# Output projection of the second attention layer: order of its first loads, and which engine forms its first remainders

## The chip, the cores and the metric

The kernel runs on one core of a Trainium2 chip. The metric is the time of one execution on the device, in microseconds. Three runs of the kernel before gave 1376.13, 1377.06 and 1377.77 us, a median of 1377.06 us. The core has a matrix engine (PE, TensorE), VectorE (DVE), ScalarE (ACT), GpSimd (POOL) and SyncE (SP, which here only issues DMAs). Each works through its own instructions in order, and they wait for one another on semaphores. Sixteen DMA engines carry the transfers of all queues.

## The reference

Two blocks over 512 tokens of width 1024. What matters here is the second layer of the first block, attention over 16 heads from shared latent keys and values, and the output projection at its end, the last line:

```python
def _mla_layer(x, w_in, q_norm, w_uq, w_out, k_nope, k_rope, v):
    b, s, _ = x.shape
    hproj = x @ w_in
    q_lat, gate = hproj[..., :Q_LORA], hproj[..., Q_LORA:]
    q = (_rms_norm(q_lat, q_norm) @ w_uq).reshape(b, s, H_B, QK_NOPE + QK_ROPE)
    q_nope = q[..., :QK_NOPE]
    q_rope = _rope(q[..., QK_NOPE:], ROPE_BASE_B)
    o = _causal_block_attention(q_nope, q_rope, k_nope, k_rope, v).reshape(b, s, WIDTH_B)
    return (o * jax.nn.silu(gate)) @ w_out
...
def first_block(x, ...):
    x = _retention_layer(...)                  # layer 0, then residual and layer norm
    x = _mla_layer(x, ..., *shared)            # layer 1, then residual and layer norm
```

A retention layer stands ahead of it. The second block behind it has a pooling mixer, neighbourhood attention and an MLP (its up and down projections).

## The kernel before

**Arithmetic.** Every fp32 operand is split in two parts: `hi`, the value rounded to the matrix engine's fp32r format, and `lo`, the remainder. A product is three matmuls, hi·hi, hi·lo and lo·hi (`split_dots`, L651 to L653). ACT rounds (`copy`, `weights_hi`, `operand_hi`), and DVE or POOL subtracts the rounded value from the original (`lo_of`, `weights_lo`, `operand_lo`, `split_lo`). So before each product a weight panel (128x2048, 1 MB) is loaded, ACT rounds it in two halves of 128x1024, and DVE or POOL forms the two remainders; the same happens to the operand from the activations (128x1024, one instruction each).

**The projections as seven products.** A large projection is done in the manner of Strassen: seven block products in place of eight, with sums of blocks as operands and sums of weight blocks as weights. The projection named `BO` (the last line of `_mla_layer`) has two panels to a product, so 14 panels, d = 0 to 13. In this text "product d" is what PE does with panel d, 24 matmuls of 512 columns. Panels 0 and 1 are plain weight blocks. Panels 2, 3 and later ones are sums of blocks, which lie ready in the DRAM tensor `tsum`.

**The sums of weights.** They are formed while attention runs: ACT copies a block into `tsum` by DMA, and POOL issues a DMA that adds another block or sum to it in DRAM (`sum_step`, issued at L872; 1 MB each, 8 KB to a packet). Each of the last sums (`DN`, for the down projection much later) waits in POOL until the sum ahead of it has landed (`add_to_sum`, which waits on `t_sum`). Of `DN`'s sums, number 10 was issued ahead of the last attention panel's remainders, in the loop over `k`, and number 11 behind the remainders of `BO`'s panel 0.

**Attention in pairs of heads.** Eight passes of `pairs`, two heads in each. A pass ends with: scores of the second head, exponentials (ACT) and normalisation (DVE); the products for the gate; the transposes of the probabilities, whose copies ACT makes as `pt_hi` and DVE as `pt_lo` (`turned`); the second head's attention on PE; the last adding up of the gate (`add_up(3)`), tanh on ACT, and the gated outputs `gt` on DVE (`gated`). SP stores `gt` to `o_spill` in DRAM (`store`). In the last pass the first operand and panel of `BO` are prepared between these steps.

**Operands of the projection.** `heads(c4)` loads four heads' outputs from `o_spill` into the tensor `bT` (1 MB) when their stores have landed. `heads(0)` and `heads(1)` serve products 0 and 1; the sums of blocks on DVE (`combine`, the tiles `comb` and `bT`) want `heads(2)` from product 4 and `heads(3)` from product 5 on. DVE waits for `heads(3)` ahead of the remainders of product 4. Stage buffers, `whi` and `wlo` rotate by three, so `seven_load` issues panel d when the remainders of panel d - 3 have been formed (`d_tlo`).

**Order on SP before.** `heads(0)`, `heads(1)`; then, when POOL has made the fourth sum of the gate (`m_ws`), panel 0; when the last attention panel's remainders are there (`w_lo`), panel 1, `heads(2)` and 1 MB of the residual `xres`; when PE has done the last gate product (`m_g`), panel 2, and panel 3 when panel 0's remainders are there; the two stores of the last pair, `heads(3)` behind them, and panels 4 to 13.

Of the kernel before, what the change touches and what calls it, by code (L numbers as in the profile page):

```python
# [32 lines left out]
PAIRS = HB // 2  # L33
# [45 lines left out]
BO = Seven(2, 14, 14, END + 8, 8, (33, 33, 33, 33), ((2, 3), (4, 5), (6, 7), (0, 1), (2, 3), (4, 5), (6, 7)))  # L79
UPN, UA = 16, 28  # L80
DN = Seven(4, UA + 2 * UPN, 28, END + 16, 16, (36, 36, 36, 40), ((0, 1), (2, 3), (4, 5), (6, 7), (0, 1), (2, 3), (4, 5)))
# [56 lines left out]
def program(nc, t, out):  # L138
    with ExitStack() as ctx:
# [7 lines left out]
        def sem(name):  # L147
            return ctx.enter_context(nc.semaphore(name))
# [175 lines left out]
        bld = xt_ld[0:4]  # L324
# [82 lines left out]
        m_s = sem("m_s")  # L407
# [54 lines left out]
        d_slo = sem("d_slo")  # L462
# [65 lines left out]
        def seven_stage(st, d):  # L528

            if st is DN:  # L530
                return third_set(d + 2)[0]
            i = own_panel(st) % 2
            return (stage[i], stage[1 - i], stage2)[d % 3]

        def seven_parts(st, d):

            if st is DN:
                hi, lo = third_set(d + 2)[1:]
            else:
                hi, lo = ((whi[0], wlo[0]), (whi[1], wlo[1]), (whi_a, wlo_a))[d % 3]  # L540
            return hi[:, 0:PAN], lo[:, 0:PAN]
# [30 lines left out]
        def seven_panel(st, f, g):  # L572

            if PLAIN[f] is None:
                return t["tsum"][st.sums + st.dq * SUMMED[f] + g, :, :]
            return block_panel(st, PLAIN[f], g)

        def block_panel(st, b, g):

            return t["w"][st.w + st.dq * b + g, :, 0:PAN]  # L580

        def sum_panel(st, i, g):

            return t["tsum"][st.sums + st.dq * i + g, :, :]
# [36 lines left out]
        def slot(x, k):  # L621

            return x[:, 512 * k:512 * k + 512]
# [35 lines left out]
        def _(sp):  # L659
# [42 lines left out]
            def seven_load(st, d):  # L702

                f, g = divmod(d, st.dq)
                if d >= 3:
                    sp.wait_ge(d_tlo, 2 * (st.at + d - 2))
                if g == 0 and SUMMED[f] is not None:
                    sp.wait_ge(t_sum, 16 * st.ready[SUMMED[f]])
                sp.dma_start(seven_stage(st, d)[:, 0:PAN], seven_panel(st, f, g)).then_inc(d_ld[(st.at + d) % 3], 16)
# [41 lines left out]
            def heads(c4):  # L751
                for e in range(2):
                    sp.wait_ge(m_st[e], 32 * (c4 + 1) + 16)
                sp.dma_start(bT[:, 4 * c4:4 * c4 + 4, :], t["o_spill"][4 * c4:4 * c4 + 4, :, :].rearrange(
                    "k p n -> p k n")).then_inc(bld[c4], 16)

            sp.wait_ge(m_kv, 4 * PAIRS)
            heads(0)
            heads(1)
            sp.wait_ge(m_ws, USED + 4 * PAIRS)  # L760
            seven_load(BO, 0)
            sp.wait_ge(w_lo, 2 * L0)
            seven_load(BO, 1)
            heads(2)
# [73 lines left out]
        def _(pool):  # L838
            def gate_sums():

                near = stage[M0 % 2]
                pool.wait_ge(landed[M0 % 2], LANDED[M0 % 2] + 16 * ((M0 + 2 - B0) // 2 + 1))
                pool.tensor_tensor(slot(near, G_S1), slot(near, G_S3), slot(near, G_S1), ADD).then_inc(m_ws, 1)
                pool.wait_ge(m_ws, USED + 1)
                pool.tensor_tensor(slot(near, G_S2), slot(near, G_S1), slot(near, G_A11), SUB).then_inc(m_ws, 1)
                pool.tensor_tensor(slot(near, G_S3), slot(near, G_A11), slot(near, G_S3), SUB).then_inc(m_ws, 1)
# [20 lines left out]
            def add_to_sum(st, i, g, src, copies, sums):  # L867

                pool.wait_ge(t_copy, 16 * (copies + 1))
                if sums:  # L870
                    pool.wait_ge(t_sum, 16 * sums)
                pool.dma_start(sum_panel(st, i, g), src, accum_op=ALU.add, max_dma_last_dim=8192).then_inc(t_sum, 16)  # L872

            def sum_step(st, i, copies, base):

                k, g = divmod(i, st.dq)
                if k == 0:
                    add_to_sum(st, 0, g, block_panel(st, 2, g), copies[0], 0)
                elif k == 1:
                    add_to_sum(st, 2, g, block_panel(st, 3, g), copies[0], 0)  # L880
                elif k == 2:
                    add_to_sum(st, 1, g, sum_panel(st, 0, g), copies[1], base + i)
                else:
                    add_to_sum(st, 3, g, sum_panel(st, 1, g), copies[1], base + i)

            def up_sum(k, g):

                pool.wait_ge(t_copy, 16 * ((12, 20)[k] + 1))
                pool.dma_start(t["usum"][k, g, :, :], t["w"][UP + g, :, 0:PAN], accum_op=ALU.add, max_dma_last_dim=8192
                               ).then_inc(t_sum, 16)  # L890

            def weights_lo(st, d):

                hi, lo = seven_parts(st, d)
                for b in range(2):
                    r = slice(b * PAN // 2, (b + 1) * PAN // 2)
                    pool.wait_ge(d_thi, 2 * (st.at + d) + b + 1)
                    pool.tensor_tensor(lo[:, r], seven_stage(st, d)[:, r], hi[:, r].bitcast(F32), ALU.subtract
                                       ).then_inc(d_tlo, 1)
# [45 lines left out]
            for k in range(4 * PAIRS):  # L945
                split_lo(M0 + k, PANEL if k % 4 == 0 else PAN)
                m = 3 * (k // 4) + k % 4
                if k % 4 == 2:
                    fourth_sum(k // 4)
                if k == 2:  # L950
                    pool.wait_ge(t_h, USED + 4)
                    pool.tensor_tensor(x_t4[1], xsum[:, 3], x_t4[0].bitcast(F32), ALU.subtract).then_inc(t_l, 1)
                if k % 4 == 3:
                    continue
                if m < 3:
                    up_sum(1, m)
                elif m == 3:
                    up_sum(1, 3)
                if 5 <= m < 13:
                    sum_step(BO, m - 5, (28, 28), 16)  # L960
                elif m >= 13:
                    sum_step(DN, m - 13, (36, 44), 24)
                if k == 0:
                    gate_sums()
            weights_lo(BO, 0)
            sum_step(DN, 11, (36, 44), 24)
            pool.wait_ge(w_lo, 2 * (L0 + 2))
            for p in range(L0 + 2, L0 + 6):
# [740 lines left out]
        def _(act):  # L1709
# [12 lines left out]
            def operand_hi(st, d):  # L1722

                f, g = divmod(d, st.dq)
                if d >= 3:
                    act.wait_ge(d_pe, st.op + d - 2)
                if SUM_OF[f] is not None:
                    act.wait_ge(d_sum, st.sums + (2 * UPN + 8 if st is DN else 0) + st.dq * SUM_OF[f] + g + 1)
                copy(operand_parts(st, d)[0], operand(st, d), d_shi)
# [318 lines left out]
            def pairs(it, last=False):  # L2048
                for s in range(2):
# [3 lines left out]
                    def c(per, k):  # L2053
                        return 2 * per * it + (per * s + k)
# [48 lines left out]
                    def next_hi(b):  # L2103
                        act.wait_ge(m_g, c(4, 7))
                        if last and s == 1:
                            if b == 0:
                                weights_hi(BO, 0)
                        else:
                            split_hi(p + 4, None, 0, PANEL, n, (b,))
# [16 lines left out]
                    for b in range(3):  # L2126
                        turned(1, b)
                    next_hi(1)
                    act.wait_ge(m_u, c(5, USED + 4))
                    tanh(0, first_t, bank[0][:, first_t])  # L2130
                    tanh(0, second_t, gate_kept[:, 0:HALF])
# [8 lines left out]

            for it in range(PAIRS // 2):
                pairs(it, it == PAIRS // 2 - 1)
            act.wait_ge(bld[1], 32)
            operand_hi(BO, 1)
            act.wait_ge(m_g, 4 * PAIRS + 4)
            weights_hi(BO, 1)
            for d in range(2, 14):
# [113 lines left out]
            for i in range(NS + 3):  # L2261
# [8 lines left out]
                if 2 <= i < NS + 2:  # L2270
                    m = i - 2
# [35 lines left out]
                if i >= 3:  # L2307
                    m = i - 3
# [102 lines left out]
        def _(dve):  # L2411
# [27 lines left out]
            def operand_lo(st, d):  # L2439

                hi, lo = operand_parts(st, d)
                dve.wait_ge(d_shi, st.op + d + 1)
                lo_of(lo, operand(st, d), hi, d_slo)
# [596 lines left out]
            def pairs(it, last=False, first=False):  # L3040
                for s in range(2):
# [90 lines left out]
                    add_up(2)  # L3132
                    for b in range(3):
                        turned(1, b)
                    if last and s == 1:
                        operand_lo(BO, 0)
                    dve.wait_ge(m_g, c(4, 8))
                    add_up(3)
                    gates(0, 0, first_t, bank[0][:, first_t])
# [11 lines left out]
                pairs(it)  # L3151
            own.leave(PAIRS // 2 - 1)
            pairs(PAIRS // 2 - 1, True)
            operand_lo(BO, 1)
            dve.wait_ge(m_g, 4 * PAIRS + 4)
            weights_lo(BO, 1)
# [103 lines left out]
            for i in range(NS + 2):  # L3260
                if i < NS:
# [5 lines left out]
                    for e in range(2):  # L3267
                        s = bank[4 + i % 2][:, e * 256:(e + 1) * 256].rearrange("p (r c) -> p r c", r=ROWS)
# [242 lines left out]
```

## Time and profile before

| | value |
|---|---|
| median of three runs | 1377.06 us (1376.13 to 1377.77) |
| the profiled execution | 1375.22 us, of which the span is 1373.1 us |
| PE busy | 1351.5 us (98%) |
| DVE busy | 1090.3 us (79%) |
| ACT busy | 766.7 us (56%) |
| POOL busy | 356.0 us (26%) |
| DMA | 265.65 MB, mean 193 GB/s |
| TensorE clock granted | 1.0 (2.4 GHz) through the span |

Times in rows are microseconds from the span's start. A row of a timeline gives the start, the duration, the engine, the line, the operation with output and input, the count, and in brackets how long the engine had been idle and what ended that. The stage of this text lies between 779 and 882 us: the end of the last pair of heads and the projection `BO`.

### The profile page before, as it was taken

What the parts mean: (1) busy time and instruction counts of PE and PEld (TensorE: products, weight loads), DVE (VectorE), ACT (ScalarE), POOL (GpSimd) and SP (SyncE); (2) the same over time, 40 slices, a digit from 0 to 9 for tenths busy, and PEclk for the clock granted to TensorE, in tenths of its full rate; (3) what the DMA queues carried; (4) which work ended last, traced back from release to release, by engine and by line L of the source; (5) the groups of instructions that cost most, each with busy time, mean ns of one, the idle gap of its engine ahead of it and who ended that gap; (6) DMA issues with size and microseconds to landing.
All of it is one profiled execution on the core that took longest, in us unless ns stands there. A gap on an engine that the chain in (4) does not pass through costs nothing. (4 is left out here: it accounts for less than half of the span.)

```text
span 1373.1 us, 19960 instructions
## 1 busy us (share of the span) xinstructions
PE 1351.5 (98%) x7596; PEld 1179.1 (86%) x7596; DVE 1090.3 (79%) x1751; ACT 766.7 (56%) x1233; POOL 356.0 (26%) x189
## 2 busy tenths in 40 slices
PE   9999999999999999999999989999999999999998
PEld 7788888888888998999899878777888999988887
DVE  7979787889967867776776689936876888889895
ACT  5453535457546444544455446648965666576554
POOL 2050414110045544544464410025304000000000
PEclk9999999999999999999999999999999999999999
DMA  6458675385377868795878797353122575456552
GB/s 270 168 177 232 192 202 186 126 281 206 132 222 180 260 212 250 226 286 119 261 231 264 201 307 295 125 205 120 66 85 78 161 212 165 150 183 213 200 190 101
DMA packets 55485, 265.65 MB, mean 193 GB/s; under 512 B 5744, under 2 KB 10480, under 8 KB 30576
## 3 DMA queue, kind: packets, MB, share of 16 engines
q1 hardware_dynamic: 38592, 166.71, 34.3%
q0 software_dynamic: 5760, 41.95, 15.6%
q10 hardware_dynamic: 11056, 55.97, 10.8%
q8 instruction: 47, 0.77, 0.2%
q14 instruction: 30, 0.25, 0.1%
HBM read 255.70 MB, written 92.80 MB: 254 GB/s over the span
## 5 line engine op out<-in xcount | busy, mean ns | idle before, releaser
L864 POOL TENSOR_TENSOR wlo<-stage,whi 128x1024 fp32r<-128x1024 f32 (+2 forms) x84 | 202.1, 2425 | 425.9 <-ACT whi L1717 339.6
L1720 ACT ACTIVATE whi<-stage 128x1024 fp32r<-128x1024 f32 (+2 forms) x155 | 148.2, 1002 | 108.0 <-PE bank L653 90.9
L2415 DVE TENSOR_TENSOR wlo<-stage,whi 128x1024 fp32r<-128x1024 f32 (+1 forms) x133 | 152.8, 1178 | 9.5 <-ACT whi L1720 9.5
L651 PE MATMUL bank<-xhi,whi 128*128 128x256 f32 (+1 forms) x428 | 133.8, 313 | 1.7 <-POOL wlo L1011 1.2
L653 PE MATMUL bank<-xhi,wlo 128*128 128x256 f32 (+1 forms) x428 | 132.9, 310 | 0.0
L652 PE MATMUL bank<-xlo,whi 128*128 128x256 f32 (+1 forms) x428 | 132.8, 310 | 0.0
L1717 ACT ACTIVATE whi<-stage 128x1024 fp32r<-128x1024 f32 (+2 forms) x90 | 89.5, 1037 | 20.2 <-issue 12.5
L651 PEld LDWEIGHTS bank<-xhi,whi 128*128 128x128 f32 x428 | 80.5, 188 | 7.2 <-DVE hid L2625 1.4
L652 PEld LDWEIGHTS bank<-xlo,whi 128*128 128x128 f32 x428 | 80.4, 188 | 5.0
L653 PEld LDWEIGHTS bank<-xhi,wlo 128*128 128x128 f32 x428 | 80.3, 188 | 5.0
L651 PE MATMUL bank<-whi,xhi 128*128 128x512 f32 (+1 forms) x204 | 78.3, 384 | 1.0 <-POOL wlo L864 0.6
L653 PE MATMUL bank<-whi,xlo 128*128 128x512 f32 (+1 forms) x204 | 77.3, 379 | 0.0
L652 PE MATMUL bank<-wlo,xhi 128*128 128x512 f32 (+1 forms) x204 | 77.2, 378 | 0.0
L913 POOL TENSOR_TENSOR wlo<-stage,whi 128x1024 fp32r<-128x1024 f32 x12 | 30.2, 2531 | 107.4 <-ACT whi L1720 107.4
L1720 ACT ACTIVATE whi<-oT 128x1024 fp32r<-128x1024 f32 x34 | 34.1, 1053 | 37.7 <-DVE oT L2876 17.9
L2090 ACT ACTIVATE prob<-bank,sm 128x512 f32<-128x512 f32 (+1 forms) x64 | 33.1, 523 | 35.1 <-DVE sm L3086 35.0
L651 PE MATMUL bank<-ql_hi,whi 128*128 128x512 f32 x120 | 47.0, 391 | 0.0
L653 PE MATMUL bank<-ql_hi,wlo 128*128 128x512 f32 x120 | 46.7, 389 | 0.0
L652 PE MATMUL bank<-ql_lo,whi 128*128 128x512 f32 x120 | 46.7, 389 | 0.0
L651 PEld LDWEIGHTS bank<-whi,xhi 128*128 128x128 f32 x204 | 38.3, 188 | 9.0 <-POOL wlo L864 1.4
L2415 DVE TENSOR_TENSOR wlo_a<-stage,whi_a 128x1024 fp32r<-128x1024 f32 x38 | 45.7, 1217 | 0.0
L653 PEld LDWEIGHTS bank<-whi,xlo 128*128 128x128 f32 x204 | 38.3, 188 | 7.0
(533 smaller groups left out, 4402.7 us busy)
## 6 DMA issues: line engine op xcount, KB each, us to landing
stage<-in_w SPq DMA_DIRECT2D x63, 1024.0 KB, 4.9
tsum<-in_w ACTq DMA_DIRECT2D x32, 1024.0 KB, 15.2
stage<-tsum SPq DMA_DIRECT2D x32, 1024.0 KB, 4.8
tsum<-in_w POOLq DMA_DIRECT2D x16, 1024.0 KB, 10.5
tsum<-tsum POOLq DMA_DIRECT2D x16, 1024.0 KB, 10.2
stage<-in_w SPq DMA_DIRECT2D x24, 512.0 KB, 4.7
stage<-in_w SPq DMA_DIRECT2D x8, 1152.0 KB, 6.2
usum<-in_w POOLq DMA_DIRECT2D x8, 1024.0 KB, 10.2
```

Source lines behind the costliest of these rows:

```text
L651: pe.matmul(dst, a_hi, b_hi, start=start, stop=False, skip_group_check=onto)
L652: pe.matmul(dst, a_hi, b_lo, start=False, stop=False, skip_group_check=onto)
L653: return pe.matmul(dst, a_lo, b_hi, start=False, stop=stop, skip_group_check=onto)
L864: pool.tensor_tensor(lo[:, to], stage[p % 2][:, r], hi[:, to].bitcast(F32), ALU.subtract).then_inc(w_lo, 1)
L913: pool.tensor_tensor(lo[:, r], a_staged(h, j)[:, r], hi[:, r].bitcast(F32), ALU.subtract).then_inc(g_plo, 1)
L1717: act.activation(parts(p)[0][:, to], stage[p % 2][:, r], ACT.Copy).then_inc(w_hi, 1)
L1720: act.activation(dst, src, ACT.Copy, scale=scale).then_inc(signal, 1)
L2090: act.activation(prob[:, at:at + w], bank[4 + q][:, 0:w], ACT.Exp, scale=-1.0, bias=sm[:, 1, 4 * e + q:4 * e + q + 1], accum_out=sm[:, 2, ...
L2415: dve.tensor_tensor(dst, src, hi.bitcast(F32), ALU.subtract).then_inc(signal, 1)
```

## The change

Four things are changed, all around the first products of `BO`.

1. SP issues the load of panel 0 between `heads(0)` and `heads(1)`, where it stood behind both.
2. The remainder of product 0's operand (`br_lo`) is formed by POOL, with a wait for the last scores of the last pair, where DVE formed it ahead of the last adding up of the gate. DVE now waits for it (`d_slo`) ahead of product 1's operand.
3. Sum 10 of `DN` is issued behind panel 0's remainders, directly ahead of sum 11.
4. ACT rounds product 1's operand ahead of the last tanh instructions, where it did so behind them.

```diff
             sp.wait_ge(m_kv, 4 * PAIRS)
             heads(0)
-            heads(1)
             sp.wait_ge(m_ws, USED + 4 * PAIRS)
             seven_load(BO, 0)
+            heads(1)
             sp.wait_ge(w_lo, 2 * L0)
             seven_load(BO, 1)
...
-                elif m >= 13:
+                elif 13 <= m < 23:
                     sum_step(DN, m - 13, (36, 44), 24)
                 if k == 0:
                     gate_sums()
+            pool.wait_ge(m_s, 8 * PAIRS)
+            operand_lo(BO, 0)
             weights_lo(BO, 0)
+            sum_step(DN, 10, (36, 44), 24)
             sum_step(DN, 11, (36, 44), 24)
...
                     next_hi(1)
+                    if last and s == 1:
+                        act.wait_ge(bld[1], 32)
+                        operand_hi(BO, 1)
                     act.wait_ge(m_u, c(5, USED + 4))
...
-            act.wait_ge(bld[1], 32)
-            operand_hi(BO, 1)
             act.wait_ge(m_g, 4 * PAIRS + 4)
             weights_hi(BO, 1)
...
-                    if last and s == 1:
-                        operand_lo(BO, 0)
                     dve.wait_ge(m_g, c(4, 8))
                     add_up(3)
...
             pairs(PAIRS // 2 - 1, True)
+            dve.wait_ge(d_slo, BO.op + 1)
             operand_lo(BO, 1)
```

How the order of instructions changes, first on POOL at the end of the attention loop. `wlo` from `stage` are remainders of weight panels, the DMA is a sum in DRAM, and the 128x512 on `stage` is the gate's fourth sum.

```order
 L864 TENSOR_TENSOR wlo<-stage,whi 128x1024 x2
 L856 TENSOR_TENSOR stage<-stage 128x512
-L872 DMA tsum<-tsum 128x2048
 L864 TENSOR_TENSOR wlo<-stage,whi 128x1024
 L864 TENSOR_TENSOR wlo<-stage,whi 128x512
+L905 TENSOR_TENSOR br_lo<-bT,br_hi 128x1024
 L898 TENSOR_TENSOR wlo<-stage,whi 128x1024 x2
-L872 DMA tsum<-tsum 128x2048
+L872 DMA tsum<-tsum 128x2048 x2
```

The sum that stood ahead of the last attention panel now stands behind the remainders of panel 0, and the operand's remainder stands ahead of them.

Then SP, at the same place of the program. `bT` are the loads of heads' outputs, `stage` the panels.

```order
 L729 DMA o_spill<-gt 128x512 x2
 L664 DMA stage<-in_w 128x1024
-L754 DMA bT<-o_spill 128x4x512 x2
-L709 DMA stage<-in_w 128x2048 x2
+L754 DMA bT<-o_spill 128x4x512
+L709 DMA stage<-in_w 128x2048
+L754 DMA bT<-o_spill 128x4x512
+L709 DMA stage<-in_w 128x2048
 L754 DMA bT<-o_spill 128x4x512
```

Panel 0 moved ahead of the second load of heads; everything behind it keeps its order.

## Rows read from the trace of the kernel before

**Rows 1.** Windows: busy us (instructions) of PE, PEld, DVE, ACT, POOL; clock; DMA share; GB/s

```profile
812.00:835.00 23.00, 22.95 (x101) 18.37 (x100) 19.96 (x18) 14.38 (x16) 0.00 (x0) 1.00 0.74 278
835.00:887.00 52.00, 49.65 (x223) 40.58 (x222) 51.38 (x65) 34.36 (x45) 0.00 (x0) 1.00 0.52 192
```

**Rows 2.** Timeline of PE, last scores to the end of the projection

```profile
790.26 0.40 PE L1383 MATMUL bank<-kr,qr 128*128 128x256 f32 x2
...
798.82 0.28 PE L653 MATMUL bank<-xhi,wlo 128*128 128x256 f32 x1
799.87 0.50 PE L651 MATMUL bank<-pt_hi,vb_hi 128*128 128x512 f32 x1 [0.77 <-DVE pt_lo L2415]
...
803.61 0.49 PE L651 MATMUL bank<-whi,br_hi 128*128 128x512 f32 x1 [1.60 <-DVE br_lo L2415]
...
810.86 0.47 PE L651 MATMUL bank<-whi,br_hi 128*128 128x512 f32 x1 [1.50 <-DVE wlo L2415]
...
881.62 1.09 PE L1078 MATMUL bank<-ident,h_tok 128*128 128x128 f32 x8 [1.88 <-DVE h_tok L2600]
```

**Rows 3.** The chain that ended last: start, us, what; first matmul of product 4

```profile
827.78 0.47 PE bank L651
```

**Rows 4.** Timeline of ACT: last exponential, panel 0, panel 4

```profile
793.78 0.20 ACT L2090 ACTIVATION_READ_ACCUMULATOR prob<-bank,sm 128x1 f32 x1
...
796.60 2.01 ACT L1720 ACTIVATE whi<-stage 128x1024 fp32r<-128x1024 f32 x2 [2.62 <-DMA stage<-in_w]
...
825.31 2.01 ACT L1720 ACTIVATE whi<-stage 128x1024 fp32r<-128x1024 f32 x2 [1.78 <-DMA stage<-tsum]
```

**Rows 5.** Timeline of DVE: product 0's operand to panel 1, and panel 4

```profile
800.66 2.89 DVE L2415 TENSOR_TENSOR br_lo<-bT,br_hi 128x1024 fp32r<-128x1024 f32 x1
803.48 0.41 DVE L3109 TENSOR_TENSOR xres<-xres,bank 128x256 f32<-128x256 f32 x1
...
807.76 0.69 DVE L3119 TENSOR_TENSOR gt<-bank,gt 128x512 f32<-128x512 f32 x1
...
809.50 2.35 DVE L2415 TENSOR_TENSOR wlo<-stage,whi 128x1024 fp32r<-128x1024 f32 x2
...
826.40 1.23 DVE L2415 TENSOR_TENSOR wlo<-stage,whi 128x1024 fp32r<-128x1024 f32 x1 [1.55 <-ACT whi L1720]
```

**Rows 6.** Timeline of POOL: sum 10, last attention panel, panel 0, sum 11

```profile
784.66 0.81 POOL L872 DMA_DIRECT2D tsum<-tsum  x1
786.88 3.84 POOL L864 TENSOR_TENSOR wlo<-stage,whi 128x1024 fp32r<-128x1024 f32 x2 [1.41 <-ACT whi L1717]
797.74 4.73 POOL L898 TENSOR_TENSOR wlo<-stage,whi 128x1024 fp32r<-128x1024 f32 x2 [7.03 <-ACT whi L1720]
802.40 0.82 POOL L872 DMA_DIRECT2D tsum<-tsum  x1
```

**Rows 7.** Timeline of SP's queue: panels 0 and 1; heads(3)

```profile
784.74 6.34 SPq L709 DMA_DIRECT2D stage<-in_w  x2
...
815.82 0.39 SPq L754 DMA_DIRECT2D bT<-o_spill  x1
```

**Rows 8.** DMA issues, KB, us to landing: panels' median; panel 0; sum 11; store; panel 4

```profile
stage<-in_w SPq DMA_DIRECT2D x63, 1024.0 KB, 4.9
...
stage<-in_w SPq DMA_DIRECT2D x1, 1024.0 KB, 11.8
...
tsum<-tsum POOLq DMA_DIRECT2D x1, 1024.0 KB, 12.2
...
o_spill<-gt SPq DMA_DIRECT2D x1, 256.0 KB, 7.3
...
stage<-tsum SPq DMA_DIRECT2D x1, 1024.0 KB, 8.4
```

**Rows 9.** DMA queues in 806 to 814: packets, MB, share of 16 engines

```profile
q0 software_dynamic: 143, 1.05, 66.9%
q1 hardware_dynamic: 336, 1.03, 33.3%
```

## The prediction

> **What bounds the kernel now.** I read the stage in four steps. First the windows: from 812 to 835 PE is busy 22.95 of 23 us and DVE 19.96; from 835 to 887 DVE is busy 51.38 of 52 and PE 49.65 [rows 1]. PE is the tighter one early in the projection and DVE is the bound later. Second, PE's own idle times: it waits 0.77 us ahead of the second head's attention, 1.60 ahead of product 0 and 1.50 ahead of product 1 [rows 2], together 3.87. From there to 879.74 it has no gap; then it waits 1.88 us for DVE [rows 2]. Third, the backward look: product 4 starts at 827.78 [rows 3], right behind DVE's first remainder of panel 4 (826.40 + 1.23 = 827.63). DVE was idle 1.55 us ahead of that one, for ACT [rows 5], and ACT was idle 1.78 us, for the panel's DMA, which landed at 825.3 [rows 4]. Behind 826.40 DVE works without a pause worth naming up to the 881.62 transposes. So the end of the projection hangs on one event, **the landing of panel 4 at 825.3**, and whatever is saved ahead of it counts only so far as panel 4 also lands earlier. Fourth, the queue of panel 4: SP issues it behind `heads(3)`, which went out at 815.82 [rows 7] and waits for the stores of the last gated outputs; the panel takes 8.4 us from its own issue [rows 8].
>
> **Panel 0 between the heads.** Issued at 784.74 [rows 7], it landed after 11.8 us [rows 8], at 796.5, behind `heads(1)` and beside sum 10, which was issued at 784.66 [rows 6]. ACT was through with its exponentials at 793.98 and stood 2.62 us [rows 4]. With neither in the way the median panel takes 4.9 us [rows 8]: 789.6, over 4 us ahead of ACT. ACT then rounds panel 0 from 793.98 to 796.0, makes `pt_hi` behind it when the transposes are there, and the 0.77 us on PE goes: the last gate product ends at 798.82 + 0.28 = 799.10 [rows 2] and attention follows. What `heads(1)` loses costs nothing: issued at 785.2 behind panel 0 it lands near 793, and ACT wants it only about 797.4, behind `pt_hi`. Should it be late by 5 us it would hold the tanh behind it.
>
> **The operand's remainder on POOL.** On DVE it took 2.89 us [rows 5], because POOL was forming panel 0's remainders (797.74 to 802.47 [rows 6]); two such halves take POOL 4.73, and so one instruction of this shape 2.4. POOL is free at 790.72 [rows 6], and the scores it now waits for end at 790.66 [rows 2], so it runs to 793.1, and panel 0's halves start at 795.1 (ACT's first half, 1.04 behind 793.98) and end at 799.8. Before, they ended at 802.47. The operand and panel are thus ready ahead of attention's end, and the 1.60 us goes. A price may arise on DVE: its normalisation of the probabilities reads SBUF while POOL's instruction runs; it begins at about 793.1 and POOL ends there, so I take 0, at most 0.4.
>
> **The gate's last adding up** stood behind the 2.89 us at 803.48 [rows 5]. Now it waits for PE's 799.10 alone: 799.3, which is 4.2 us earlier, with tanh, the gated outputs (the last from 807.76 [rows 5] to 803.6) and their stores behind it. DVE starts panel 1's remainders at 805.4 in place of 809.50 [rows 5], has the first half at 806.6, and product 1 can start at 810.86 - 3.87 = 806.99: the 1.50 us goes too. ACT's operand for product 1, one instruction of 1.04, now lies in the 1.5 us in which ACT waits for the adding up, and costs nothing. **So the first four products run 3.87 us earlier**, and PE comes to product 4 at about 823.8.
>
> **The sums.** Sum 10 leaves 784.66 and is issued at 799.8, and sum 11, which has to wait for its landing, follows at 799.8 + 12.2 = 812.0 where it stood at 802.40 [rows 6, 8]. What a sum costs the others: from 806 to 814 its queue q0 held 66.9% of the 16 engines, 5.35 us, and SP's q1 with 33.3% moved 1.03 MB in 8 us [rows 9]. So a sum is paid with 5.35 us of everybody's transfers. Before, both were over by 814.6 and nothing ran against `heads(3)` and panel 4. Now sum 11 runs from about 815 to 823, over exactly these.
>
> **What panel 4 does then.** Its time is the issue of `heads(3)`, plus 9.5 us (825.3 - 815.82), plus what the sum takes. The issue moves up with the stores' landing. The second store was issued at 808.5 and took 7.3 us [rows 8], since it queued behind panel 3 and shared with sum 11. DVE's shift is 4.2; the shift of the sum beside panel 3 is 802.40 - 799.8 = 2.6. Its bounds are these two; I take 3.0, near the lower end, because the landing is governed by panel 3 and the sum, and the loads ahead of them drain a little sooner. Then the sum: 5.35, with 0 as its other end if it hides in the pause between stores and `heads(3)`. Together -3.0 + 5.35 = **+2.35 us**: panel 4 lands near 827.7, product 4 starts at 830.1, and PE waits 6 us for it. The 3.87 us gained is waited away there, and 2.35 more. DVE behind it has no pause in which to catch up.
>
> The Trainium skill ("DMA: Bandwidth & Descriptors", the section on queues, rings and completion order) says that an engine takes turns between queues packet by packet. In this trace 336 packets of q1 and 143 of q0 carried the same 1.03 and 1.05 MB, so small packets got less than their share of bytes [rows 9], which agrees. By the rule `heads(3)`, made of 2 KB rows, would be nearly stopped while the sum's 8 KB packets pass, and the sum of terms would be the same +2.35, with no hope of the sum giving way.
>
> **Sum against the profiled execution.** It took 1375.22 us; 1375.22 + 2.35 = 1377.6. The median stands 1.84 higher, so I forecast **1379.4**. A measurement of this kernel can tell about 0.2%, 2.75 us, so below 1374.3 is faster and above 1379.8 slower. The forecast lies inside, near the slower edge.
>
> **Rivals.**
> 1. *The sum costs panel 4 nothing.* Sum 11 would have to slip into the pause, or give way to SP's queue. Then panel 4 is 2.6 to 3.9 us earlier (PE's own gain is the upper end): 1373.2 to 1374.5, typically 1374.0. For it: transfers are pausing between the last store and `heads(3)`. Against it: sum 11 starts moving some 3 us behind its issue, and q0 took two thirds of the engines when it did run [rows 9]. Chance 0.14.
> 2. *Half of it hides.* The sum costs 2 to 4 us: 1375.5 to 1378.3. Chance 0.20.
> 3. *Forecast.* 1378.3 to 1379.8. Chance 0.38.
> 4. *Slower, by the stall itself.* PE stands idle 6 us ahead of product 4. In the trace before no gap of PE here exceeds 1.88 us and the granted clock is 1.00, its upper level of 2.4 GHz [rows 1, 2]. If the clock fell to 1.2 GHz in the gap, product 4 would take 11 us in place of 5.5 at worst, against the 1.88 us that PE waits for DVE at the end: up to 3.6 us more, and I take 1.5. It decides as soon as a part of more than one third of a product runs slow. The same end is reached if the stores land no earlier (shift 0: +5.35). 1379.8 to 1382.4. Chance 0.24. The Trainium skill ("TensorE: Matmul & The Clock Gate", its practical guidance) says that idle gaps between bursts bring the clock to the lower level and asks to avoid them; no row here shows such a fall.
> 5. *The change doesn't do what it says at the front* (panel 0 still late, or POOL's instruction blocks DVE's normalisation and PE waits at the transposes). The end still hangs on panel 4, whose loads are delayed as above or, with later stores, more: 1377 to 1381. Chance 0.04.
>
> **Numbers.** Faster: most of rival 1, 0.12. Slower: rival 4, and a part of the forecast's upper edge and of rival 5, 0.33. Within 0.2%: 0.55. The range of 8 in 10 takes in most of rival 1 at the bottom and most of rival 4 at the top: 1374.0 to 1381.6. The likeliest case alone has 1378.3 to 1379.8.
>
> **What would show it.** Right at the front: PE's gaps of 0.77, 1.60 and 1.50 us gone, product 1's start at 807.0, POOL's `br_lo` at about 790.9, the last adding up near 799.3. Right behind it: `heads(3)` issued near 812.8, sum 11 issued near 812, panel 4's landing near 827.7, a single PE gap of about 6 us ahead of product 4, and the transposes 2.35 us later, near 884. Wrong: if the gap is below 3 us, the sum's cost is mis-sized; if there's no gap and the transposes come at 878 to 879, rival 1 holds; a granted clock under 1.00 behind the gap speaks for rival 4. A sum 11 issued later than 820 would also void the collision.

## The result and the profile after

| | before | after |
|---|---|---|
| median | 1376.68 us (22 runs) | 1378.69 us (22 runs) |
| ratio after to before | | 1.0018, 95% interval 1.0010 to 1.0027 |
| the profiled execution | 1375.22 us, span 1373.1 | 1379.77 us, span 1377.6 |
| mean granted clock | 1.000 | 0.995 |

The change makes the kernel slower by 0.18%, some 2.5 us. The profiled execution of the kernel after lies 1.1 us above its median and that of the kernel before 1.5 us below its own, so the two traces stand 4.5 us apart where the medians stand 2.0. So a difference of 1 to 2 us between two single traces can be the spread of executions alone. The trace after also runs 0.76 us late before the change can act: `heads(0)` is issued at 780.31 in place of 779.55. Where a time of after is compared with one of before, this is taken off ("corrected"), and so is the like offset of every other trace.

PE first, with the idle time ahead of an instruction in brackets. It has only one long pause from the scores to the transposes at the projection's end:

```profile
833.19 0.76 PE L651 MATMUL bank<-whi,br_hi 128*128 128x512 f32 x1 [9.04 <-DVE wlo L2419]
```

The three waits of [rows 2], 0.77, 1.60 and 1.50 us, are gone. In their place stands one of 9.04 us, ahead of product 4. Who is waited for there is seen on ACT (panel 4) and on DVE (the last adding up, product 4's operand, panel 4):

```profile
830.73 2.00 ACT L1723 ACTIVATE whi<-stage 128x1024 fp32r<-128x1024 f32 x2 [10.82 <-DMA stage<-tsum]
```

```profile
799.90 0.42 DVE L3113 TENSOR_TENSOR xres<-xres,bank 128x256 f32<-128x256 f32 x1 [1.12 <-PE bank L653]
...
826.97 1.23 DVE L2419 TENSOR_TENSOR br_lo<-bT,br_hi 128x1024 fp32r<-128x1024 f32 x1 [7.08 <-DMA bT<-o_spill]
...
831.82 1.23 DVE L2419 TENSOR_TENSOR wlo<-stage,whi 128x1024 fp32r<-128x1024 f32 x1 [3.62 <-ACT whi L1723]
```

ACT no longer waits for panel 0 (it stood 2.62 us in [rows 4] and now starts on it at 794.64, right behind the exponentials) but stands 10.82 us for panel 4 (1.78 before). DVE's adding up waits for PE alone and comes at 799.14 (corrected) in place of 803.48 [rows 5]. Then DVE stands 7.08 us for `heads(3)` and 3.62 us for panel 4. The chain that ended last (start, us, what) has the transfer itself in it, which it hadn't before:

```profile
817.54 13.16 DMA stage<-tsum
```

POOL and SP's queue show how it came to that:

```profile
791.50 2.40 POOL L905 TENSOR_TENSOR br_lo<-bT,br_hi 128x1024 fp32r<-128x1024 f32 x1
...
800.47 0.81 POOL L872 DMA_DIRECT2D tsum<-tsum  x1
815.88 0.84 POOL L872 DMA_DIRECT2D tsum<-tsum  x1 [14.61 <-DMA tsum<-tsum]
```

```profile
802.35 2.85 SPq L729 DMA_DIRECT2D o_spill<-gt  x2
816.51 0.39 SPq L754 DMA_DIRECT2D bT<-o_spill  x1
```

The stores are issued some 4 us earlier, yet `heads(3)` goes out at 815.75 (corrected), where it stood at 815.82 [rows 7]. Sum 10, now issued at 800.47, needed 14.9 us to land. Sum 11 follows at 815.88, 0.6 us ahead of `heads(3)`, and runs with it. Queues from 817.4 to 824.5 (packets, MB, share of the 16 engines):

```profile
q0 software_dynamic: 143, 1.05, 81.1%
q1 hardware_dynamic: 181, 0.37, 17.3%
```

Sum 11 held the engines for 5.8 us (81.1% of 7.1), and SP's queue moved 0.37 MB, most of it `heads(3)`, beside it.

Product 4 starts at 833.19, corrected 832.4, which is 4.65 us later than the 827.78 of [rows 3], and the transposes at 886.7 (corrected) in place of 881.62. Between the two DVE has no slack. From its first remainder of panel 4 (826.40 in [rows 5], 831.82 above) to this row, an instruction of the layer norm behind the projection, it takes 50.85 us before and 50.84 after:

```profile
877.25 1.28 DVE L2593 SCALAR_TENSOR_TENSOR xres<-h_tok,small,rows 128x1024 f32<-128x1024 f32 x1
```

```profile
882.66 1.28 DVE L2597 SCALAR_TENSOR_TENSOR xres<-h_tok,small,rows 128x1024 f32<-128x1024 f32 x1
```

In all ten traces of this text the distance is 50.83 to 50.85 us. So what the stage takes is decided by the time at which DVE starts on panel 4.

### The profile page after: what moved, and what is told of

Same layout as the page of the kernel before. It is cut to its first block, busy times and chain, and to the rows that moved or that the text cites. A ratio compares the mean times of both kernels' runs of the same rounds, so it can differ in the third digit from the quotient of the medians.

```text
span 1377.6 us, 19963 instructions
## 1 busy us (share of the span) xinstructions
PE 1352.2 (98%) x7596; PEld 1179.6 (86%) x7596; DVE 1087.7 (79%) x1750; ACT 767.1 (56%) x1233; POOL 358.4 (26%) x190
## 4 chain that ended last, share of the span: by engine, by line
PE 76%; DVE 15%; DMA 3%; ACT 3%; issue 1%; POOL 1%; SPq 0%; ACTq 0%; DVEq 0%; POOLq 0%
PE bank L651 22%; PE bank L652 22%; PE bank L653 22%; DVE wlo L2419 3%; PE bank L1500 3%; PE bank L1386 3%; PE bank L1414 1%; DMA stage<-in_w 1%; DVE wlo_a L2419 1%; DMA stage<-tsum 1%; POOL wlo L864 1%; DMA v_spill<-v_tok 1%; DVE xres L2481 1%; DVE xlo L2419 1%; DVE ar_lo L2419 1%
```

## The experiments

Each was timed against the kernel before on the same chip, the "a" kernels together and the "b" kernels together on another chip. "a" kernels start from the changed kernel, "b" kernels from the kernel before. Ratios can be compared across the groups, medians only inside one.

| kernel | ratio to before | 95% interval | median us |
|---|---|---|---|
| the change | 1.0018 | 1.0010 to 1.0027 | 1378.69 |
| a1, its sums as before | 0.9990 | 0.9981 to 1.0000 | 1375.77 |
| a3, its sum 11 late | 0.9980 | 0.9967 to 0.9992 | 1374.34 |
| a2, both its sums late | 0.9945 | 0.9932 to 0.9959 | 1368.73 |
| a4, filler matmuls | 1.0015 | 1.0003 to 1.0027 | 1379.12 |
| b1, panel order only | 1.0001 | 0.9989 to 1.0013 | 1377.22 |
| b2, operand on POOL only | 1.0002 | 0.9989 to 1.0015 | 1377.98 |
| b3, sum 10 moved only | 1.0019 | 1.0005 to 1.0032 | 1379.08 |
| b4, both sums late only | 0.9957 | 0.9942 to 0.9972 | 1371.27 |

The theory: the transfers are the bound from 781 us on, and the moved sums collide with `heads(3)` and panel 4. The rivals: the new order of loads and remainders is itself the cost; the clock's fall behind the stall is the cost.

### The sums back in their places (a1)

```diff
-                elif 13 <= m < 23:
+                elif m >= 13:
...
             weights_lo(BO, 0)
-            sum_step(DN, 10, (36, 44), 24)
             sum_step(DN, 11, (36, 44), 24)
```

> The changed kernel with the two weight sums where they were before the change: sum 10 ahead of the last attention panel's remainders, sum 11 behind panel 0. Theory (the sums' transfers beside heads(3) and panel 4 cost the time): nothing runs beside heads(3) and panel 4 any more; panel 0 shares with sum 10 but lands near 794, still in time; PE's waits of 0.77, 1.60 and 1.50 us stay gone, heads(3) goes out 2.6 to 4.2 us earlier than before the change, no long gap of PE ahead of product 4: 2.6 to 3.9 us faster than before the change, ratio 0.9972 to 0.9981. Rival (the new order of loads and of remainders is itself the cost, the sums are bystanders): the gap of PE ahead of product 4 stays above 5 us and the ratio stays at 1.001 to 1.003. Second rival (sum 10 spoils panel 0 and with it the front): panel 0 lands behind 796, a PE wait of 1 to 3 us comes back ahead of product 0, ratio 0.9985 to 1.0.

It was 0.10% faster than before (the interval ends at 1.0000) and 0.28% faster than the changed kernel. The intervals of these two do not overlap, so the order of loads and remainders is not the cost, and the sums' place is; the first rival falls. But the theory gave 0.19% to 0.28% against before, and its trace was to show `heads(3)` 2.6 to 4.2 us earlier. `heads(3)` goes out at 817.42, corrected 817.2 and so 1.35 us later than in the trace before, PE pauses 0.53 us ahead of product 4, and nothing is gained at the transposes (883.0 corrected). The second rival has the right range of the ratio, but not the right place: panel 0 was in time. PE has a wait that the theory did not name, ahead of product 2:

```profile
816.10 0.47 PE L651 MATMUL bank<-whi_a,s_hi 128*128 128x512 f32 x1 [3.67 <-DVE wlo_a L2418]
```

ACT had waited 3.67 us for panel 2 itself, up to 813.64. In the kernel before, panel 2 landed at 806.6. What sum 10 leaves to SP's queue while it runs differs. First the kernel before (787.6 to 796.1, sum 10 beside panels 0 and 1), then a1 (789.1 to 795.8, sum 10 beside `heads(1)`):

```profile
q0 software_dynamic: 143, 1.05, 61.5%
q1 hardware_dynamic: 185, 1.39, 40.1%
```

```profile
q0 software_dynamic: 143, 1.04, 78.9%
q1 hardware_dynamic: 233, 0.45, 21.4%
```

The sum moves packets of 8 KB, a panel too, `heads(1)` packets of 2 KB. With panel 0 ahead of `heads(1)`, it is `heads(1)` that shares with the sum, and SP's queue gets 0.45 MB through in place of 1.39. Panels 1 and 2 queue behind it, and sum 11, issued 2.7 us sooner (corrected), now meets panel 2 also. The panel's place saves at the front and costs in the queue. A second cost of the same edit lies in SP's waits: `heads(1)` now stands behind the wait for the gate's fourth sum and goes out at 785.4, where `heads(0)` and `heads(1)` went out together from 779.55. From 781 to 785 the DMA engines are busy 69% of the time in place of 93%.

### Both sums late (a2), and sum 11 alone late (a3)

```diff
             weights_lo(BO, 0)
+            pool.wait_ge(d_tlo, 2 * (BO.at + 13))
             sum_step(DN, 10, (36, 44), 24)
             sum_step(DN, 11, (36, 44), 24)
```

In a3 the wait stands between the two sums.

> The changed kernel with both sums issued only when the remainders of the projection's 13th panel are formed (about 871 us), so none runs beside panels 0 to 7. Theory: panel 3 and the stores land without a sum beside them, near 807 and 808, heads(3) goes out near 808 in place of 815.8, panel 4 lands near 818, in time: PE's waits are gone up to the end of the projection, 3.9 us faster than before the change, ratio 0.9972, bounded by the front's gain on PE and DVE. If the sums then collide with the loads of the next stage, up to 3 us of it are given back. Rival (order of loads is the cost): ratio 1.001 to 1.003 as in the changed kernel.

> The changed kernel with sum 11 alone deferred to the remainders of the projection's 13th panel; sum 10 stays behind panel 0. It tells the two sums apart. Theory: sum 10 still slows panel 3 and the stores, so heads(3) goes out at 813 to 815.8, but panel 4 then takes 9.5 us from there as before the change: product 4 starts 0 to 3 us earlier than before the change, ratio 0.998 to 1.0; the gap of PE ahead of it is 1 to 4 us. If sum 10 is the whole cost: ratio above 1.0015. If sum 11 is the whole cost and the stores do land 3 us earlier: ratio 0.998.

With both late the kernel is 0.55% faster than before, twice what was expected. `heads(3)` goes out 7 us earlier (809.39, of which 0.53 is an offset of this trace), panel 4 lands in time, and PE has no pause up to the transposes:

```profile
876.15 1.09 PE L1082 MATMUL bank<-ident,h_tok 128*128 128x128 f32 x8 [0.55 <-DVE h_tok L2605]
```

The transposes come at 875.6 (corrected) against 881.62 [rows 2], 6.0 us earlier. DVE starts on panel 4 at 820.94, corrected 820.4, in place of 826.40: the same 6.0. The "bound by the front's gain" in the expectation was wrong. With panel 4 in time, DVE starts on it earlier than the 3.87 us of the front, and its 50.84 us of work from there end that much earlier. PE's wait at the end shrinks from 1.88 to 0.55.

With sum 11 alone late, the pause ahead of product 4 is small:

```profile
826.06 0.47 PE L651 MATMUL bank<-whi,br_hi 128*128 128x512 f32 x1 [2.32 <-DVE wlo L2420]
```

`heads(3)` goes out at 814.10 (0.31 offset), 2.0 us earlier than before, and ACT starts on panel 4 at 823.60, 9.5 us behind it, as in the kernel before. (This trace is of the fastest execution of a3, 2.3 us under its median.) So each sum has its own price. Sum 10 beside panel 3 and the stores costs 5.6 us (1374.34 less 1368.73, timed together). Sum 11 beside `heads(3)` and panel 4 costs 5.2 us by the ratios (1.0018 less 0.9980), and 4.4 by the medians of two groups. By the intervals each of the two is uncertain by some 2 us.

### Filler in PE's gap (a4)

```diff
+                if d == 3:
+                    pe.wait_ge(m_gt, 3 * PAIRS + 3)
...
+                    for i in range(28):
+                        last = pe.matmul(bank[0][:, :], operand_parts(BO, 3)[0][:, 0, 0:P], kept_hi[:, 0, :], start=True,
+                                         stop=True)
```

> The changed kernel with 28 extra matmuls of 512 columns (6.3 us) behind product 3, into a bank that product 6 overwrites; they fill most of PE's gap ahead of product 4 and nothing reads them. It measures what the granted clock's fall behind that gap (0.5 of full speed for 10 us in the profile of the changed kernel) costs the kernel. Theory (DVE bounds the stage from panel 4 on, PE had 1.9 us in hand at its end): the clock stays at 1.00, product 4 takes 5.5 us in place of 8, and the time falls by 0 to 0.7 us against the changed kernel, ratio to before 1.001 to 1.002. Rival (the clock is the cost of the stall): the time falls by 1.5 to 3 us, ratio 0.9995 to 1.0005.

In the changed kernel the clock was at 0.50, 1.2 GHz, for the first 5.2 us behind the gap (columns as in [rows 1], the clock behind POOL's busy time):

```profile
833.30:838.50 5.20, 5.20 (x13) 4.03 (x14) 5.15 (x5) 3.92 (x5) 0.00 (x0) 0.50 0.66 250
```

With the filler it stayed at 1.00:

```profile
832.00:838.00 6.00, 5.89 (x26) 4.90 (x27) 5.95 (x6) 4.05 (x6) 0.00 (x0) 1.00 0.58 201
```

PE still paused 1.76 us between the filler and product 4. And the time was the same: ratios 1.0015 and 1.0018, medians 1379.12 and 1378.69. The timing alone could not settle a price of 1.5 us, since the interval of a4 reaches down to 1.0003, and the rival began at 1.0005. The traces settle it. DVE's way from panel 4 to the layer norm is 50.84 us in the trace after, with the clock at 0.50, and 50.85 us in a4 (830.74 to 881.59) and before, with the clock at 1.00. PE does lose time in the trace after: it reaches the transposes 0.5 us behind DVE, for which it had waited 1.88 us before. But the product behind the transposes waits for DVE again. So the clock's fall is real and costs this kernel nothing, because DVE bounds the stage from there on; the second rival falls.

### The parts alone (b1, b2, b3)

```diff
             heads(0)
-            heads(1)
             sp.wait_ge(m_ws, USED + 4 * PAIRS)
             seven_load(BO, 0)
+            heads(1)
```

> The kernel before with one edit: panel 0 is loaded between heads(0) and heads(1). Theory (from 781 us to the landing of the last stores the DMA engines are the bound; every load and both sums lie ahead of heads(3), so an order within them moves nothing at its end): the wait of 0.77 us goes, DVE's remainder of product 0's operand still waits for POOL (now to about 800), product 1 starts some 2 us earlier, heads(3) still goes out at 815 to 817, ratio 0.999 to 1.001. Rival (panel 0's late landing was what the kernel lost): 2 to 2.7 us faster, ratio 0.998 to 0.9985.

```diff
+            pool.wait_ge(m_s, 8 * PAIRS)
+            operand_lo(BO, 0)
             weights_lo(BO, 0)
...
-                    if last and s == 1:
-                        operand_lo(BO, 0)
...
+            dve.wait_ge(d_slo, BO.op + 1)
             operand_lo(BO, 1)
```

> The kernel before with one edit: POOL forms the remainder of product 0's operand and DVE waits for it ahead of product 1's operand. Theory: panel 0 still lands at 796.5, so POOL's remainders of it stay at 797.7 to 802.5; the wait of 1.60 us ahead of product 0 shrinks to 0 to 0.5, the last adding up moves up by 2 to 4 us, but sum 11, panel 3 and the stores keep their landing, heads(3) goes out at 815 to 816 and product 4 starts as before: ratio 0.9993 to 1.0007. Rival (DVE's 2.89 us were on the path): 1.6 to 3 us faster, ratio 0.998 to 0.9988.

```diff
-                elif m >= 13:
+                elif 13 <= m < 23:
...
             weights_lo(BO, 0)
+            sum_step(DN, 10, (36, 44), 24)
             sum_step(DN, 11, (36, 44), 24)
```

> The kernel before with one edit: sum 10 is issued behind panel 0's remainders, directly ahead of sum 11. Theory: panel 0 lands near 792, in time; the front gains 0.8 to 3 us; sum 10 runs beside panel 3 and the stores, sum 11 beside heads(3) and panel 4, which lands 3 to 5 us later than before; a gap of PE of 4 to 8 us ahead of product 4: the whole loss of the changed kernel is here, ratio 1.001 to 1.003. Rival (the loss came from the other parts): ratio 0.998 to 1.0.

The first two cannot be told from before: ratios 1.0001 and 1.0002, intervals of 0.13% to either side at most. Neither of the waits that they save ends last. In b1 product 1 starts 2.6 us earlier than before, and then PE waits 1.90 us at product 2 and 2.12 us at product 4. `heads(3)` goes out at 817.1 and in b2 at 816.7 (corrected), 1.3 and 0.9 us later than in the trace before and at or just above the upper end of what was expected. In b2 loads and sums keep their order, so 0.9 us is also what one execution can differ from another; and PE's pause ahead of product 4 is 3.22 us there. The windows (columns as in [rows 1]) show what the panel's place does to the DMA engines, b1's below that of the kernel before. Their share of busy time can come out a little over 1:

```profile
781.00:795.00 14.00, 14.00 (x110) 13.66 (x109) 12.73 (x46) 8.62 (x23) 8.14 (x5) 1.00 1.01 312
```

```profile
781.00:795.00 14.00, 14.00 (x110) 13.65 (x109) 12.74 (x46) 9.53 (x25) 8.25 (x6) 1.00 0.86 240
```

The third has the whole loss of the change, 1.0019 against 1.0018. The gap ahead of product 4 is there, and ACT starts on panel 4 14.05 us behind the issue of `heads(3)` (813.79 to 827.84), where a3 and the kernel before have 9.5:

```profile
830.30 0.76 PE L651 MATMUL bank<-whi,br_hi 128*128 128x512 f32 x1 [5.29 <-DVE wlo L2416]
```

### Both sums late, nothing else (b4)

The edit of a2 in the kernel before, with sum 10 taken out of the loop.

> The kernel before with one edit: both sums are issued when the remainders of the projection's 13th panel are formed (about 871 us). The other three parts of the change are absent. Theory (DMA bound): the front's wait of 0.77 us goes by itself since panel 0 lands near 790, DVE's operand remainder and its wait for POOL remain, heads(3) goes out near 809 to 811 and panel 4 lands in time: 3.5 to 6 us faster than before, ratio 0.9955 to 0.9975, and 2 to 4 us slower than the changed kernel with both sums late (0.9945), which is what the other three parts are worth once the queue is free. Rival (the sums' removal does everything and the other parts nothing): the same time as that kernel, ratio 0.994 to 0.995.

0.43% faster than before, as expected. This edit has none of the other three parts, and DVE starts on panel 4 4.3 us earlier than before. `heads(3)` goes out at 808.38. Of the front's three waits only the last is left, since panel 0 now lands in time without any new order:

```profile
808.12 0.47 PE L651 MATMUL bank<-whi,br_hi 128*128 128x512 f32 x1 [1.54 <-DVE wlo L2417]
```

The changed kernel with both sums late does not have this wait, and its ratio is lower by 0.0012, some 1.7 us. But the two were not timed together and their intervals overlap, so that the other three parts are worth anything, once the queue is free, is indicated and not shown. The best kernel of the study is a2, 0.55% faster than before.

## Why the prediction was right, point by point

The time, 1378.69, lies in the range and 0.7 us from the forecast of 1379.4, on the side of the forecast and inside the band of 0.2%. The mechanism held: a sum that meets `heads(3)` and panel 4, a pause of PE ahead of product 4, a loss behind a front that is faster. That the number came so close is partly luck, since one of its two terms was too favourable and the kernel regained some time behind the stage (below). Its base was a little off too: over 22 runs the median of the kernel before is 1376.68, 0.4 us under the 1377.06 of three runs.

**The event that decides.** That the stage hangs on panel 4's landing held. In all eight traces in which ACT waits for panel 4, product 4 starts 2.5 us behind ACT's start on it, and where the panel landed in time (a2, b4) PE ran through.

**The front.** It held to a few tenths. The three waits are gone; `br_lo` on POOL took 2.40 us and stood at 790.7 (corrected; forecast 790.9); the adding up came at 799.14 (forecast 799.3); DVE's normalisation was not held up by POOL. The 3.87 us were gained and waited away again, as said.

**The sum beside panel 4.** Forecast at 5.35 us. From the issue of `heads(3)` to ACT's start on panel 4 it is 9.47 to 9.50 us in the five traces without the sum there (before, a1, a3, b1, b2) and 14.22 with it, 15.21 in a4's trace and 14.05 in b3's: 4.6 to 5.7 us. The term had the right size. The prediction's reading of [rows 9], that the small packets got less than their share of bytes, does not come out of that row, where both queues moved about the same. Over the sum's own time in the trace after (817.4 to 824.5) it holds, with 0.37 MB against 1.05, though `heads(3)` was slowed there and not stopped.

**The issue of `heads(3)`.** This is the term that was mis-sized. The prediction took 3.0 us earlier, between bounds of 2.6 and 4.2. The traces of the changed kernel and of a4, which are the same program up to there, gave 0.1 and 2.0 (814.44, less an offset of 0.60), and a3 and b3 gave 2.0. The bounds had been taken from the shift of DVE and of the sum, but the second store lands when the transfers ahead of it are through. Before, two sums were among these, after only sum 10, so 5.35 us of transfers fewer; and yet the issue moved by 2.0 at most. The rest is engine time that the new order leaves idle at its start, where sum 10 used to run:

```profile
781.00:795.00 14.00, 14.00 (x108) 13.60 (x107) 12.73 (x45) 8.89 (x24) 10.54 (x6) 1.00 0.79 284
```

A share of 0.79 in place of 1.01 over 14 us is 3.1 us of transfers not made there (2.8 in b3, whose share is 0.81). Taken off the 5.35 us it leaves 2.3 to 2.6, near the 2.0 of three traces. That is an estimate from these windows, and no run separates it. The trace after, with 0.1, is the odd one: its sum 10 took 14.9 us to land, against 12.9 in a4 and b3 and 12.2 assumed.

With 2.0 in place of 3.0 the sum of terms would be +3.35 and the forecast 1380.4; the measured median is 1.7 us lower than that. In the traces product 4 starts 4.65 us later than before (after), 3.7 (a4) and 2.6 (b3), where +2.35 was forecast, and the transposes come at 886.7, 885.4 and 884.3, where 884 was forecast. At the end of the span these three are only 3.7, 2.3 and 1.1 us later than before (corrected), 2.4 on the mean, which agrees with the medians' +2.0 and the ratio's +2.5. The stage loses more than was forecast, and part of it comes back behind the stage: in the trace after PE's wait ahead of L1500 (L1497 in the kernel before), at some 940 us, is 0.58 us in place of 1.50. The forecast took the stage's loss for the kernel's. That the two errors nearly cancel is luck, and why that wait shrinks stays open.

**The gap and the clock.** A gap of about 6 us was forecast, and 9.04 was there in the trace after; in b3's, whose front gains less, it was 5.29. The clock fell, as rival 4 had it, to half speed; matmuls of 512 columns took 628 ns in the place of 389. But its price of 1.5 us was not there, as a4 and DVE's unchanged 50.84 us show. The prediction had rightly named what absorbs it, the 1.88 us that PE has in hand at the end, and should have taken 0 and not 1.5. The Trainium skill ("TensorE: Matmul & The Clock Gate", the section "Why this matters for your kernels") asks to have no long idle gaps of PE between bursts of matmuls, since they bring the clock back to its lower level. The trace agrees as to the clock (0.50 behind the gap of 9.04 us); the kernel's time did not follow it.

**Rival 1**, that the sum costs nothing, is refuted by b3 and by a1 against the change. **Rival 5** did not occur.

## What to carry to other kernels

A transfer that is moved out of one engine's way is paid for where it lands: before moving it, list what is in the queues at its new place and which of these loads the bounding engine waits for. Where the DMA engines are full over a stretch, a new order within it moves waits about and can leave engine time unused at its start, so that it ends no sooner; here only traffic taken out of the stretch moved its end much. The same two sums, put where the DMA engines were busy some 60% of the time, turned a loss of 0.18% into a gain of 0.55%. And an idle engine's waits at the front are worth nothing until the one event behind which the bound engine never pauses comes earlier too.

## What the runs showed of the hardware

Two queues that want the same DMA engines get about as many packets through, whatever their size. From 819 to 822 in the trace after, sum 11 moved 57 packets and SP's queue 60; from 790 to 795 in a1 sum 10 moved 100 and SP's queue 97. Beside a sum of 8 KB packets SP's queue moved 1.39 MB in 8.5 us when it held panels of 8 KB packets, and 0.37 to 0.45 MB in about 7 us when it held loads of 2 KB packets. So which load meets a sum decides how far the queue behind it comes. In a1 panel 2 came 7 us later than before; how much of the missing gain is due to that and how much to the idle time ahead of it was not separated. The Trainium skill ("DMA: Bandwidth & Descriptors", the section on queues, rings and completion order) says that an engine takes turns between queues by packets, and these counts agree with it; the price for a queue of small packets is from these rows.
